# Experts' matrices in seven slots, pairs written out, each scatter behind the next pair's gate product

## The reference

```python
def moe_ffn(h, w_router, b_router, w_gate, w_up, w_down):
    ...
    idx, wts = route(x2, w_router, b_router)
    ...
    def expert_block(args):
        xb, e = args
        return (jax.nn.silu(xb @ w_gate[e]) * (xb @ w_up[e])) @ w_down[e]

    ys = lax.map(expert_block, (xs, block_expert)).reshape(cap, D)
    y = jnp.zeros((T, D), h.dtype).at[buf_tok].add(ys * buf_w[:, None].astype(ys.dtype))
    return y.reshape(B, S, D)
```

## Time and profile before

| | us |
|---|---|
| median of 3 runs (lowest, highest) | 2595.56 (2591.27, 2597.82) |
| the profiled execution, its own time | 2602.74 |
| its span, first to last instruction | 2600.9 |
| first layer of experts, first gate product to last scatter's start | 455.79 to 721.92 |
| second layer, the same | 940.31 to 1207.76 |
| TensorE busy in the whole span | 2381.2 (92%) |

### The profile page before, as it was taken

One profiled execution on the slowest core, in us unless ns is written; L12 is line 12 of the kernel. 1 busy time (PEld: TensorE's weight loads), 2 busy tenths in 40 slices (PEclk: granted clock), 3 DMA queues, 4 the chain that ended last, 5 costly groups with the idle time before them and its releaser, 6 DMA issues.

```text
span 2600.9 us, 34034 instructions
## 1 busy us (share of the span) xinstructions
PE 2381.2 (92%) x13194; PEld 1806.7 (69%) x13194; DVE 1219.7 (47%) x2258; ACT 927.4 (36%) x1644; POOL 114.1 (4%) x96
## 2 busy tenths in 40 slices
PE   6998998889889988897999988999999999899999
PEld 4875577444347754443788867988888887699887
DVE  4522235000032330002776366677777737567776
ACT  3431211100022220001654464464555444555543
POOL 0000000000000000000000520000000034000000
PEclk8999998999989989998999999999999999899999
DMA  9858841899932349996466241546656634144663
GB/s 319 315 182 301 316 161 65 337 373 380 363 139 89 127 165 373 369 376 238 148 191 204 100 162 52 178 143 196 191 160 201 189 125 162 66 159 143 189 186 100
DMA packets 306460, 535.62 MB, mean 206 GB/s; under 512 B 12638, under 2 KB 198688, under 8 KB 294048
## 3 DMA queue, kind: packets, MB, share of 16 engines
q1 hardware_dynamic: 305388, 532.61, 58.0%
q10 hardware_dynamic: 948, 1.28, 0.2%
HBM read 532.81 MB, written 1.05 MB: 205 GB/s over the span
## 4 chain that ended last, share of the span: by engine, by line
PE 79%; DVE 9%; DMA 6%; ACT 3%; issue 2%; SPq 0%; ACTq 0%; DVEq 0%
PE bank L582 14%; PE bank L848 12%; PE bank L978 12%; PE yacc L882 9%; PE bank L853 6%; PE bank L566 4%; DMA wring<-in_moe_w_down 4%; PE bank L617 2%; PE yacc L778 2%; PE yacc L1015 2%; PE bank L939 2%; PE yacc L599 2%; PE bank L1197 1%; PE yacc L1141 1%; PE bank L646 1%
## 5 line engine op out<-in xcount | busy, mean ns | idle before, releaser
L978 PE MATMUL bank<-wring,arena 128*64 128x512 f32 x1536 | 355.1, 617 | 50.7 <-issue 32.6
L848 PE MATMUL bank<-h_split,w_hi 128*128 128x512 f32 x1408 | 352.3, 392 | 0.0
L2168 DVE TENSOR_TENSOR w_lo<-wring,w_hi 128x1024 fp32r<-128x1024 f32 x264 | 307.2, 1217 | 10.7 <-ACT w_hi L1542 10.7
L978 PEld LDWEIGHTS bank<-wring,arena 128*64 128x64 f32 x1536 | 122.5, 142 | 263.7 <-issue 259.0
L1542 ACT ACTIVATE w_hi<-wring 128x1024 fp32r<-128x1024 f32 x264 | 277.3, 1055 | 49.0 <-PE yacc L882 49.0
L848 PEld LDWEIGHTS bank<-h_split,w_hi 128*128 128x128 f32 x1408 | 259.3, 189 | 50.0
L1360 ACT ACTIVATE arena<-bank 128x256 f32<-128x256 f32 (+2 forms) x330 | 116.6, 377 | 342.7 <-PE bank L582 124.4
L1508 ACT ACTIVATE arena<-bank 128x512 f32<-128x512 f32 x76 | 43.9, 596 | 487.0 <-PE bank L978 293.1
L853 PEld LDWEIGHTS bank<-h_split,w_lo 128*128 128x128 f32 x1408 | 194.0, 192 | 20.0 <-DVE h_split L2210 5.5
L853 PE MATMUL bank<-h_split,w_lo 128*128 128x256 f32 x1408 | 199.6, 285 | 5.3 <-DVE h_split L2210 5.3
L2718 POOL TENSOR_TENSOR wx_lo<-wring,wx_hi 128x1024 fp32r<-128x1024 f32 x42 | 107.6, 2563 | 2112.4 <-ACT wx_hi L1400 2112.4
(11 more groups left out here) (387 smaller groups left out, 3721.7 us busy)
## 6 DMA issues: line engine op xcount, KB each, us to landing
wring<-in_ffn_w_in SPq DMA_DIRECT2D x176, 512.0 KB
wring<-in_moe_w_gate SPq DMA_DIRECT2D x32, 2048.0 KB
wring<-in_moe_w_up SPq DMA_DIRECT2D x32, 2048.0 KB
wring<-in_moe_w_down SPq DMA_DIRECT2D x32, 2048.0 KB
wring<-in_w_ada SPq DMA_DIRECT2D x28, 2048.0 KB
wring<-in_ffn_w_out SPq DMA_DIRECT2D x88, 512.0 KB
wring<-in_w_in SPq DMA_DIRECT2D x20, 2048.0 KB
wring<-in_a_w_in SPq DMA_DIRECT2D x8, 2048.0 KB
```

The lines of the kernel that those rows point to most:

```text
L848: return mm(b[:, :], r(w_hi[:, j % 2, g, c * HB:(c + 1) * HB]), r(h_split[:, c, :, :].rearrange("p a t -> p (a t)")), start=start, stop=st ...
L978: last = mm(b[e * SLOTS:(e + 1) * SLOTS, :], x[:, k, e * SLOTS:(e + 1) * SLOTS], w[e][:, k, cols], start=(k == 0), stop=(k == n - 1), skip ...
L2168: tt(w_lo[:, j % 2, part, :].bitcast(F32R), wring[:, (u0 + j) % WSLOTS, part * DC * HB:(part + 1) * DC * HB], w_hi[:, j % 2, part, :], ALU ...
```

## The change

It does three things in the two layers of experts.

- **Seven slots.** The 48 units of a layer go round seven slots: the four of `wring`, and three pieces of `arena` (`MOE_EXTRA`: columns 10496 to 14592, 14592 to 18688, and 6400 to 10496). Each slot has a semaphore of its own, `moe_landed`. Unit n waits for unit n-7. The first four units wait for the ring's slots as before; units 4 and 5 wait for the last `head_ready` (in the second layer, for the last attention output `moba.o14`), unit 6 for the last `y0_summed` (`y1_summed`). The last readers of the ring's four slots are now pair 7's gate product (two slots) and up product (two slots), so the loads of the part behind wait for those.
- **Pairs written out.** `all_pairs` calls `pair` for all eight pairs on PE, ACT, DVE and SP; the loops go.
- **The scatter moved.** On PE the scatter of pair p-1, with its wait for S, d0 and d1 to be copied out, stands between pair p's gate product and its up product. The last pair's scatter stands behind its down products as before. Banks and their order stay; ACT's and DVE's orders stay.

```diff
-PAIR_LOOP = (1, PAIRS // 2 - 1)
+MOE_SLOTS = 7
+MOE_EXTRA = (10496, 14592, 6400)
...
+        moe_landed = [sem(f"moe_landed{i}") for i in range(MOE_SLOTS)]
...
-        def all_pairs(eng, pair):
...
+        def all_pairs(pair):
+
+            for p in range(PAIRS):
+                pair(p // 2, p % 2)
...
+        def moe_slot(l, n):
+
+            j = n % MOE_SLOTS
+            if j < WSLOTS:
+                return wring[:, (moe_first[l][0] + j) % WSLOTS, 0:D * FE // P]
+            return arena[:, MOE_EXTRA[j - WSLOTS]:MOE_EXTRA[j - WSLOTS] + D * FE // P]
...
+        def moe_unit_used(l, n):
+
+            p, m = divmod(n, PAIR_UNITS)
+            return pair_full(l, p // 2, p % 2, ("g", "u", "d1")[m // 2])
...
+                moe_first.append((len(tags), freed[-WSLOTS:]))
...
+                def scatter(i, odd):
+
+                    first, last_pair = (2 * i + odd == p for p in (0, PAIRS - 1))
+                    for step in ("S", "d0", "d1"):
+                        pe.wait_ge(*pair_drained(l, i, odd, step))
+                    for m in range(DC):
+                        if last_pair and m and m % 2 == 0:
+                            last.then_inc(part_scattered, 1)
+                        last = mm(ysum(m), ye[:, m * P:(m + 1) * P], S_e, start=first and m % 2 == 0,
+                                  stop=last_pair and m % 2 == 1, skip_group_check=True)
+                    last.then_inc(scattered, 1)
...
                     for n, step in enumerate(("g", "u")):
                         w = [unit(i, odd, 2 * n + e, DC, FE) for e in range(2)]
                         done(i, odd, step, halves(take(i, odd, step), XG, DC, w, slice(0, FE)))
+                        if n == 0 and not first:
+                            scatter(*divmod(2 * i + odd - 1, 2))
...
-                all_pairs(pe, pair)
+                all_pairs(pair)
+                scatter(PAIRS // 2 - 1, 1)
...
+                for j in range(WSLOTS):
+                    freed[j - WSLOTS] = moe_unit_used(l, range(j, PAIRS * PAIR_UNITS, MOE_SLOTS)[-1])
...
+            arena_left = [((head_ready.sem, NH), (head_ready.sem, NH), (y0_summed, NH * (DC // 2))),
+                          (full("moba.o14"), full("moba.o14"), (y1_summed, DC * (DC // 2)))]
...
+                        if n < WSLOTS:
+                            sp.wait_ge(*moe_first[l][1][n])
+                        elif n < MOE_SLOTS:
+                            sp.wait_ge(*arena_left[l][n - WSLOTS])
                         else:
...
+                            sp.wait_ge(*moe_unit_used(l, n - MOE_SLOTS))
+                        src, e = mats[m // 2], 4 * i + 2 * odd + m % 2
+                        sp.dma_start(moe_slot(l, n).rearrange("p (k n) -> p k n", k=src.shape[2]),
+                                     src[:, e:e + 1, :, :].rearrange("p e k n -> p (e k) n")) \
+                            .then_inc(moe_landed[n % MOE_SLOTS], 16)
```

More of the change, by code:

```diff
@@ L378, in pair_drain_sem, with moe_unit_landed @@
             return bank_drained[pair_use(l, i, odd, step)[0]]
-        def all_pairs(eng, pair):
[L382 to L388, removed]
+        def all_pairs(pair):
+            for p in range(PAIRS):
+                pair(p // 2, p % 2)
+        moe_first = []
+        def moe_slot(l, n):
[3 more added lines that the diff above has]
+            return arena[:, MOE_EXTRA[j - WSLOTS]:MOE_EXTRA[j - WSLOTS] + D * FE // P]
+        def moe_unit_landed(l, n):
+            j = n % MOE_SLOTS
+            return moe_landed[j], 16 * (l * len(range(j, PAIRS * PAIR_UNITS, MOE_SLOTS)) + n // MOE_SLOTS + 1)
+        def moe_unit_used(l, n):
+            p, m = divmod(n, PAIR_UNITS)
+            return pair_full(l, p // 2, p % 2, ("g", "u", "d1")[m // 2])
         split = {}
@@ L955, in moe @@
                 filled(f"over{l}", mm(b[0:1, 0:1], sm[:, 264:265], ones[:, 0:1], start=True, stop=True))
-                u0, k0 = len(tags), len(uses)
+                k0 = len(uses)
                 uses[f"moe{l}.g0"] = k0
+                moe_first.append((len(tags), freed[-WSLOTS:]))
                 def unit(i, odd, n, k, cols):
-                    u = u0 + PAIR_UNITS * odd + n
-                    pe.wait_ge(w_landed[u % WSLOTS], i * (48 * 2 * PAIR_UNITS // WSLOTS) + 48 * (u // WSLOTS + 1))
-                    return wring[:, u % WSLOTS, 0:k * cols].rearrange("p (k n) -> p k n", k=k)
+                    n += PAIR_UNITS * (2 * i + odd)
+                    pe.wait_ge(*moe_unit_landed(l, n))
+                    return moe_slot(l, n).rearrange("p (k n) -> p k n", k=k)
                 def take(i, odd, step):
@@ L980, in halves @@
                     return last
+                def scatter(i, odd):
[8 more added lines that the diff above has]
+                    last.then_inc(scattered, 1)
                 def pair(i, odd):
-                    first, last_pair = (isinstance(i, int) and 2 * i + odd == p for p in (0, PAIRS - 1))
+                    first, last_pair = (2 * i + odd == p for p in (0, PAIRS - 1))
                     for n in range(2):
@@ L1023, in moe @@
                         uses[f"moe{l}.{step}{p}"] = len(uses) if (step, p) != ("g", 0) else k0
-                    for n in range(PAIR_UNITS):
-                        tags.append(f"moe{l}.{p}.{n}")
-                        freed.append(pair_full(l, i, odd, ("g", "u", "d1")[n // 2]))
+                for j in range(WSLOTS):
+                    freed[j - WSLOTS] = moe_unit_used(l, range(j, PAIRS * PAIR_UNITS, MOE_SLOTS)[-1])
                 last_uses = sorted(uses.values())[-4:]
@@ L1516, in pair @@
                     move(i, odd, "d1", ye[:, 512:D])
-                all_pairs(act, pair)
+                all_pairs(pair)
                 act.wait_ge(flagged, l + 1)
@@ L2143, in pair @@
                         .then_inc(pair_drain_sem(l, i, odd, "d0"), 1)
-                all_pairs(dve, pair)
+                all_pairs(pair)
                 dve.wait_ge(flagged, l + 1)
@@ L2559, in pair @@
                 def pair(i, odd):
[L2560 to L2576 removed]
+                    for m in range(PAIR_UNITS):
+                        n = PAIR_UNITS * (2 * i + odd) + m
+                        if n < WSLOTS:
+                            sp.wait_ge(*moe_first[l][1][n])
+                        elif n < MOE_SLOTS:
+                            sp.wait_ge(*arena_left[l][n - WSLOTS])
+                        else:
+                            sp.wait_ge(*moe_unit_used(l, n - MOE_SLOTS))
[3 more added lines that the diff above has]
+                            .then_inc(moe_landed[n % MOE_SLOTS], 16)
+                all_pairs(pair)
                 sp.wait_ge(flagged, l + 1)
```

19 lines of the change are left out of this document (2 added, 17 removed).

## The result

The median falls from 2593.41 us (4 runs) to 2521.95 us (4 runs, 2518.79 to 2527.15), ratio 0.9726, 95% interval 0.9701 to 0.9751. A second set on another occasion gave 0.9730 (0.9714 to 0.9745).

A forecast was written before the change was run, and what follows sets the result against it. The prediction took the ring of four slots as the bound, with DMA and TensorE waiting for each other. Layer gains of 32.8 and 34.1 us, 66.9 together, less 2.0 gave 64.9: from 2595.56 to 2531 us, range 2519 to 2562.

The forecast's parts named there:

- The bound of before: Expert layers: four slots run dry, DMA and TensorE wait for each other; first-layer matrix waits 9.3 and 15.2 us.
- The scatter moved: Seven of eight scatters per layer lose their 0.78 us wait for ACT's copy of d1: gain 5.5 us per layer.
- the third rival: The change doesn't do what it says: arena loads run no earlier, starved pairs give back 0.78; near 2595, chance 0.04.
- A layer as TensorE alone runs it: Expert layer rebuilt from TensorE's steps, pairs 1 to 6 at 29.83: 233.3 us, gaining 32.8 and 34.1, together 66.9.
- Can the transfers follow: Whether DMA keeps up in the expert layers: 5.07 to 5.39 us a unit, break-even 5.26, TensorE setting the end.
- the prediction's formula: Last unit lands 9.8 + 41 x u us into the layer, u being time per unit; TensorE wants it at 225.4.
- the charge of 2 us: Deducted for both expert layers together, as TensorE and DMA come out nearly level.
- DMA sets the pace: Rival: in the expert layers the last unit lands 13.2 us late; gain 40.5, 2555 us; chance 0.24.
- What lies behind: Stretch behind each expert layer: earlier loads gain nothing; norm gaps of 3.66 and 2.77 us may move -3 to +3, taken as 0.
- Pairs written out: Expert pair loops removed: turns' ends show no gap, 621.56 being cited; more code to fetch; effect 0.
- The sum: Whole kernel: 66.9 - 2.0 = 64.9 us gained, 2595.56 to 2530.7, rounded to 2531.
- Instruction fetch takes the wait's place: Rival: each of 16 written-out pairs stops for fetch and loses 4.5 us, 72 in all; 2603 us; chance 0.04.

The follow-up runs named there:

- the second execution: The changed kernel itself profiled and measured once more, nothing edited, on the same chip as the others of its set: 2525.25 us, ratio 0.9730 to before.
- the kernel with the scatter at the transposes: Changed kernel with the previous pair's scatter between transposes hT and S (last pair: ahead of hT): 2515.79 us, 0.9692; with next part's loads held 2500.9 us, 0.9640.

## Why the prediction held, and where it did not

- **The bound of before**: right. Waits for matrices were 24.5 us of the first layer, 0.6 of them ahead of the first gate product; with seven slots only those 0.6 are left.
- **The scatter moved**, 5.5 us a layer: measured 5.8 beside seven slots (238.7 against 232.9). "Cost nothing" was right. Beside four slots the layers were 4.7 and 3.6 us shorter, with 23 us of waits left, so the rule in the third rival, that a starved pair gives it back, was at most right in part.
- **A layer as TensorE alone runs it**, 233.3 us: 234.6 and 232.9. The pairs' 29.83 were 29.77. The gain of 66.9 was 66.0. "No product should start cold" failed once: the last down products of the first layer took 8.78 us behind waits of 1.20 and 0.67. In the second layer, and in both layers of the second execution, they took 7.09 behind the same waits.
- **Can the transfers follow**: yes. The unit of 5.07 to 5.39 us was too slow at both ends. With queued work it is 2.097 MB at 421 GB/s, 4.98 us, which by the prediction's formula puts the last unit at 214, 11 ahead of TensorE; at 5.19 it was 3. The readings of 5.19 and 5.39 were taken where a queue ran dry. So the charge of 2 us was nothing, the rival "DMA sets the pace" did not come about, while 12.5% more bytes brought it in; nothing between was tried. The HBM Reference of the Trainium skill (Specifications) gives about 425 GB/s for a core that streams alone. The row's 421 agrees with it, and the 358 for a shared pair does not apply to this run.
- **What lies behind**, "earlier loads gain nothing" and "between -3 and +3 per layer, taken as 0": this term of the sum was mis-sized. It was 9.9 and 4.3 us, 14.2 together (10 in the second execution). The prediction had seen the two gaps and their neighbours, branch and loads, but took them as noise around 0 instead of working out what the changed order of loads does to them. The four loads now go out a product earlier and end at the very time of the branch. Held back, they free 12 us of the kernel before by themselves.
- **Pairs written out**, 0: right for the layers (0.9994), but it did take the hole of 2.77 us and what followed from the first norm, 5.6 us. The prediction took the product at 621.56 for one behind a turn's end. It is pair 5's, inside the second turn; pair 4's at 589.41 does stand behind a turn's end, and has no gap either.
- **The sum**: 64.9 forecast, 79.0 between the profiled spans. 14.2 of the difference are the stretches behind, 2.0 the charge, -0.9 the layers, and -1.3 the untouched parts (4.5 lost, 3.0 and 0.2 gained). Between the medians the gain was 71.5, 6.6 over the forecast. That the point came so near owes something to luck: of the 10 to 14 us that the forecast missed behind the layers, only a part shows between the medians, and no run says what took the rest.
- **Instruction fetch takes the wait's place**: no stop in any written-out pair. Nine instruction packets came in the changed kernel's first layer, none with a wait of its own behind it. A wait of 3 to 4 us at a branch beside traffic was real, at the one place of each layer that has a branch. Runtime: NRT & Kernel Launch of the Trainium skill (Instruction fetch mechanics) says that code in sequence is fetched ahead, and that a taken branch to code outside the part already fetched has to wait for a fetch. The traces agree on both: no stop in the written-out pairs, and a packet ahead of each wait behind the branch over the general path. The loop's jump back of before, at 589.41, cost nothing, and from 571 to 658 us no instruction packet came at all.

What stays open: shown is that the wait behind the layer needs the flag's read and branch and grows with transfers in flight, and that it ends a steady 2.4 to 2.9 us behind the start of an instruction packet. Why that packet starts later beside traffic isn't shown: the flag may be read later, or the fetch asked for later. The reading of the flag was not taken away alone. Nor was the shorter first layer in the kernel without the general path followed up.

## What to carry to other kernels

Give a stream of equal loads as many slots as keep it from running dry, and then look for what the next bound is; here the fifth slot did it, and arena space that was dead in this phase paid for it. A step that doesn't depend on a copy is best put where TensorE waits for it, and that is worth more than the gap's length in the trace (1.14 us for 0.72). Prefetches for the part behind a branch should be over before it or start after it: keep them out of the few microseconds in which TensorE jumps.

## What the runs showed of the hardware

- One core's 16 DMA engines read 417 to 427 GB/s for 170 to 190 us on end while TensorE was busy 97 to 100% of the time, and TensorE's products stayed at 7.09 us beside them.
- Filling a gap that the trace shows as 0.72 us on TensorE shortened its cadence by 1.14 us: 0.70 at the place of the gap, the rest in the records around it.
- Behind the branch over the path that isn't taken, TensorE waited 0.4 to 1.3 us in quiet and 1.9 to 4.1, mostly over 3.2, while loads ran, and then most column sums ran partly at 1.2 GHz (mostly 5.38 instead of 3.69 us). The wait ended 2.4 to 2.9 us behind the start of a 16 KB instruction packet, which started 2.7 and 3.3 us later beside traffic (the kernel with the scatter at the transposes, loads not held, against held).
- The granted clock fell for one product (8.78 us instead of 7.09; 0.85 and 0.81 in the windows from 675 to 685 us) behind waits of only 1.20 and 0.67 us, in the first layer of the changed kernel and of the one with five slots. In no second layer, and not in the changed kernel's second execution, did it fall behind such waits, so they alone don't decide it.
